# Row maxima of a sparse-attention block: the key products of the maximum pass on half the contraction rows

## The reference

```python
o_cmp, p_cmp = compressed_attention(q, kc, vc, scale)     # 63 compressed keys
sel_idx = select_blocks(p_cmp, s_len)                     # 16 of 16 blocks: all of them
o_slc = selected_attention(q, k_s, v_s, sel_idx, scale)   # causal over all keys
o_win = window_attention(q, k_w, v_w, scale)              # causal, last 512 keys
```

## Time and profile before

| | |
|---|---|
| median of 3 runs | 992.6 us (991.83 to 993.16) |
| the profiled execution | 991.09 us, its span 989.3 us |
| granted TensorE clock, mean | 0.987 |
| PE busy | 910.2 us (92%), 5573 products |
| DVE busy | 528.5 us (53%) |
| ACT busy | 394.5 us (40%) |
| chain that ended last, by engine | PE 71%, DVE 14%, ACT 6%, SP queue 3% |
| maximum pass | first product at 308.8 us, last at 594.0 us |

### The profile page before, as it was taken

One profiled execution on the slowest core, in us unless ns is written; L12 is line 12 of the kernel. 1 busy time (PEld: TensorE's weight loads), 2 busy tenths in 40 slices (PEclk: granted clock), 3 DMA queues, 4 the chain that ended last, 5 costly groups with the idle time before them and its releaser, 6 DMA issues.

```text
span 989.3 us, 14340 instructions
## 1 busy us (share of the span) xinstructions
PE 910.2 (92%) x5573; PEld 745.6 (75%) x5581; DVE 528.5 (53%) x1075; ACT 394.5 (40%) x786; POOL 215.7 (22%) x213
## 2 busy tenths in 40 slices
PE   0799999899999999999998998889999999999996
PEld 0488999689999766666676766678888888877885
DVE  1561279426765487797786876552231222217543
ACT  5533232422123466767657667641111111114121
POOL 6249512111100112212203212145551000000000
PEclk9999999899999999999999999989999999999998
DMA  9917041031010000000000001043322112033222
GB/s 314 356 44 128 4 111 65 1 88 45 1 44 1 2 1 1 1 1 1 2 1 1 1 2 32 7 123 96 100 71 70 53 33 59 16 154 127 87 85 85
DMA packets 53716, 59.67 MB, mean 60 GB/s; under 512 B 10097, under 2 KB 45489, under 8 KB 52609
## 3 DMA queue, kind: packets, MB, share of 16 engines
q1 hardware_dynamic: 51392, 54.13, 18.3%
q0 software_dynamic: 2000, 4.54, 1.6%
q10 hardware_dynamic: 256, 0.09, 0.0%
HBM read 52.92 MB, written 5.24 MB: 59 GB/s over the span
## 4 chain that ended last, share of the span: by engine, by line
PE 71%; DVE 14%; ACT 6%; SPq 3%; issue 3%; DMA 2%; POOL 0%; DVEq 0%; ACTq 0%; POOLq 0%
PE bank L1588 39%; PE slc_max L1588 15%; PE win_max L1588 13%; PE bank L1591 3%; DVE plo L1142 3%; SPq L488 2%; DVE rt L1142 2%; DVE mx L1410 2%; DMA ada<-in_w_ada 2%; ACT pt L815 1%; DVE mx L1417 1%; ACT phi L815 1%; ACT osb L815 1%; DVE qa L1142 1%; SPq L527 1%
## 5 line engine op out<-in xcount | busy, mean ns | idle before, releaser
L1142 DVE TENSOR_TENSOR plo<-pt,phi 128x512 fp32r<-128x512 f32 x192 | 116.2, 621 | 36.8 <-ACT phi L815 36.4
L815 ACT ACTIVATE pt<-bank 128x512 f32<-128x512 f32 (+1 forms) x208 | 98.7, 474 | 83.3 <-PE bank L1588 77.2
L1588 PE MATMUL bank<-q,k 128*128 128x512 f32 (+7 forms) x384 | 102.7, 349 | 0.9
L815 ACT ACTIVATE phi<-bank 128x512 fp32r<-128x512 f32 (+1 forms) x208 | 98.5, 474 | 0.0
L601 POOL TENSOR_TENSOR qa<-qa,otmp 128x256 f32<-128x256 f32 x32 | 27.5, 859 | 215.2 <-DVE otmp L1142 215.2
L1588 PEld LDWEIGHTS bank<-q,k 128*128 128x128 f32 (+1 forms) x384 | 63.4, 190 | 11.9 <-ACT phi L815 2.9
L1588 PE MATMUL bank<-phi,vhi 128*65 128x512 f32 x192 | 70.1, 365 | 2.4 <-ACT osb L815 1.9
L1588 PE MATMUL bank<-phi,vlo 128*64 128x512 f32 x192 | 62.0, 323 | 0.0
L1588 PE MATMUL bank<-plo,vhi 128*65 128x512 f32 x192 | 61.9, 323 | 0.0
L1588 PE MATMUL bank<-ht_hi,dhi 128*128 128x512 f32 x128 | 50.6, 396 | 2.8 <-DVE at_lo L1142 2.8
L1410 DVE TENSOR_REDUCE mx<-slc_max 128x1 f32<-128x128 f32 (+3 forms) x64 | 48.1, 752 | 8.7 <-PE slc_max L1588 8.7
(11 more groups left out here) (395 smaller groups left out, 2535.8 us busy)
## 6 DMA issues: line engine op xcount, KB each, us to landing
ada<-in_w_ada SPq DMA_DIRECT2D x8, 1024.0 KB, 17.0
draw<-in_w_in SPq DMA_DIRECT2D x16, 512.0 KB, 3.9
wraw<-in_w_in SPq DMA_DIRECT2D x7, 1024.0 KB, 5.4
xs<-in_x SPq DMA_DIRECT2D x8, 512.0 KB, 10.9
gstage<-in_w_ada POOLq DMA_DIRECT2D x16, 256.0 KB, 3.1
oraw<-in_w_out SPq DMA_DIRECT2D x8, 512.0 KB, 6.5
xr<-in_x SPq DMA_DIRECT2D x8, 512.0 KB, 4.3
out<-yr SPq DMA_DIRECT2D x8, 512.0 KB, 2.9
```

Of the source, the lines that this page charges most:

```text
L815: return nc.scalar.activation(o, i, fn, **kw)
L1142: return V.tensor_tensor(o, a, b, op)
L1588: return T.matmul(o, l, r, start=start, stop=stop, **kw)
```

## The change

The products of the maximum pass contract 64 rows instead of 128, that is query high part times key high part, without the key's low part. So that selected and window keys lie on different rows, the window keys' high part goes to slot 1 of `kcat` and their low part to slot 0: of the window's `k1`, rows 64 to 127 hold the high part. The copy into `k2` then reads rows 64 to 127 for the window. "MX" and "MW" become one step: both waits first, then in turn a selected product on rows 0 to 63 and a window product on rows 64 to 127, each in its own bank, then the masks of the selected keys (signal `ms`), the window's masks, the compressed mask, and the compressed product with all 128 rows last (signal `mw`). The "MW" entries stay in the plan; TensorE does nothing at them.

```diff
--- before.py
+++ after.py
@@ -1070,7 +1070,7 @@
                 act.wait_ge(once("krot"), m + 1)
                 if m >= 2:
                     act.wait_ge(s_tr, key_fill(m - 2) + 1)
-                a(kcat[m % 2][:, :, 0, :], rt1[:, 0:P].rearrange("p (g d) -> p g d", g=GROUPS))\
+                a(kcat[m % 2][:, :, m // ST, :], rt1[:, 0:P].rearrange("p (g d) -> p g d", g=GROUPS))\
                     .then_inc(once("khi"), 1)
                 if m >= 2:
                     key_high(m - 2)
@@ -1469,7 +1469,7 @@
                 dve.wait_ge(s_tr, fl + 1)
                 dve.wait_ge(once("k1"), m + 1)
                 V.tensor_copy(k2[b][0:HD, :, P * i:P * i + P],
-                              bank[fl % 2][0:HD, 0:2 * P].rearrange("p (g s) -> p g s", g=GROUPS))\
+                              bank[fl % 2][HD * b:HD * b + HD, 0:2 * P].rearrange("p (g s) -> p g s", g=GROUPS))\
                     .then_inc(s_trf, 1)
 
             for m in range(2 * ST):
@@ -1491,8 +1491,8 @@
                 dve.wait_ge(once("krot"), m + 1)
                 dve.wait_ge(once("khi"), m + 1)
                 kc_ = kcat[m % 2]
-                tt(kc_[:, :, 1, :], rt1[:, 0:P].rearrange("p (g d) -> p g d", g=GROUPS),
-                   f(kc_[:, :, 0, :]), ALU.subtract).then_inc(once("klo"), 1)
+                tt(kc_[:, :, 1 - b, :], rt1[:, 0:P].rearrange("p (g d) -> p g d", g=GROUPS),
+                   f(kc_[:, :, b, :]), ALU.subtract).then_inc(once("klo"), 1)
                 if m >= 2:
                     key_rows(m - 2)
                 if m == 2:
@@ -1888,27 +1888,21 @@
                     lhs = q1[h % 2][:, P * i:P * i + P]
                     if n >= 1:
                         pe.wait_ge(once("msr"), n)
-                    for s0 in range(0, i + 1, 4):
-                        s1 = min(s0 + 4, i + 1)
-                        mm(slc_max[:, P * s0:P * s1], lhs, k1[0][:, g, P * s0:P * s1], True, s1 != i + 1)
-                    mm(slc_max[:, P * i:P * i + P], identb[:, :], maskb[:, 0, :], False, True).then_inc(once("ms"), 1)
-                elif step[0] == "MW":
-                    _, h, i = step
-                    n, g = max_no(h, i), h // HPG
-                    lhs = q1[h % 2][:, P * i:P * i + P]
-                    buf = win_max
-                    if n >= 1:
                         pe.wait_ge(once("mwr"), n)
                     j0 = max(0, i - WIN_TILES)
                     cnt = i + 1 - j0
-                    for s0 in range(0, cnt, 4):
-                        s1 = min(s0 + 4, cnt)
-                        mm(buf[:, P * s0:P * s1], lhs, k1[1][:, g, P * (j0 + s0):P * (j0 + s1)], True, False)
+                    for s0 in range(0, i + 1, 4):
+                        s1, w1_ = min(s0 + 4, i + 1), min(s0 + 4, cnt)
+                        mm(slc_max[:, P * s0:P * s1], lhs[0:HD], k1[0][0:HD, g, P * s0:P * s1], True, s1 != i + 1)
+                        if s0 < cnt:
+                            mm(win_max[:, P * s0:P * w1_], lhs[HD:P], k1[1][HD:P, g, P * (j0 + s0):P * (j0 + w1_)],
+                               True, False)
+                    mm(slc_max[:, P * i:P * i + P], identb[:, :], maskb[:, 0, :], False, True).then_inc(once("ms"), 1)
                     if i >= WIN_TILES:
-                        mm(buf[:, 0:P], identb[:, :], maskb[:, 1, :], False, True)
-                    mm(buf[:, P * (cnt - 1):P * cnt], identb[:, :], maskb[:, 0, :], False, True)
-                    mm(buf[:, 640:704], lhs, k1c[:, g, 0, :], True, False)
-                    mm(buf[:, 640:704], identb[:, :], cmpq[:, i, :], False, True).then_inc(once("mw"), 1)
+                        mm(win_max[:, 0:P], identb[:, :], maskb[:, 1, :], False, True)
+                    mm(win_max[:, P * (cnt - 1):P * cnt], identb[:, :], maskb[:, 0, :], False, i < WIN_TILES)
+                    mm(win_max[:, 640:704], identb[:, :], cmpq[:, i, :], i < WIN_TILES, False)
+                    mm(win_max[:, 640:704], lhs, k1c[:, g, 0, :], False, True).then_inc(once("mw"), 1)
                 elif step[0] == "MM":
                     h, hf = step[1:]
                     pe.wait_ge(once("mcat"), 2 * (h + 1))
```

## The result

The median became 997.57 us (996.80 to 999.44) against 992.63 us for the kernel before, four runs each: ratio 1.0052, interval 1.0036 to 1.0068. The change costs 4.9 us, where 1.7 were forecast; the time lies inside the prediction's range (989.0 to 998.0) and outside the likeliest case's own (992.0 to 996.5). The profiled execution took 998.23 us, its span is 996.4, 7.1 us longer than before.

What follows compares the result with a forecast made beforehand. TensorE was taken as busy 35.96 of 38.65 us a head, alternating with VectorE on the chain. Heads +1.4 and opening +0.3 took 991.1 to 992.8 us; 1.5 more gave 994.3, range 989.0 to 998.0.

Steps and rivals of the forecast that it cites:

- likeliest case: The forecast of 994.3 us for the whole kernel, with its own range 992.0 to 996.5 and chance 0.60.
- The half form on TensorE: Maximum pass: two halves take the time of one, switches take 0.23 to 0.29 us back; tiles 4 to 7 -0.09 to -0.10.
- state-space rows: Trace rows of 64-row products in the state-space stage: two halves overlap fully, entering costs 0.19 us behind a plain product.
- Rival (a): Switches beside bf16 masks are cheaper: 986.6 us if they cost nothing, 990.5 half way; chance 0.17.
- The merged wait at tile 7: Tile 7's selected products also wait for tile 6's window maxima; TensorE's next columns come 0.34 us later a head.
- The slack on VectorE: VectorE's 0.54 us wait near 474.8 absorbs selected signals 0.2 us later, and output transposes find bank 7 free.
- Rival (b): VectorE's queue passes the later signal on: 0.22 us at tile 3, 0.23 at tile 4, 997.5 us; chance 0.18.
- Tile 2 was put under cover: Tile 2's +0.06 us on TensorE costs nothing, lying inside the VectorE stretch that ends at 463.93.
- The opening: Head 0's tiles, between projection blocks: plain entries on TensorE and later tiles waiting for maxima, together +0.3 us.
- The key preparation: Eight copies reading rows 64 to 127 and writing rows 0 to 63 cost 0; +3.3 us without VectorE's free time.
- The sum: Seven heads at +0.2 us give +1.4, with the opening's +0.3 making +1.7 us in all.
- that 1.5 us: The whole kernel's median before, 992.6 us, lay 1.5 above its profiled execution; the forecast added this to 992.8.

Runs made afterwards that it cites:

- e4_new45: The changed kernel with the half-height form at tiles 4 and 5 alone, all other tiles as before; 993.76 us against 991.99, ratio 1.0018.
- e1_waits: The kernel before with only the wait for the window maxima moved ahead of the first selected product; 997.91 us against 992.16, ratio 1.0073.
- e3_old67: The changed kernel with tiles 6 and 7 as before (128 rows, separate waits); 993.19 us against 992.16, ratio 1.0016.
- e2_signal: The kernel before; at tiles 0 to 5 the selected maxima's signal comes with the first window product; 997.04 us, ratio 1.0052; rerun 998.30 us, ratio 1.0056.
- e5_same_rows: The changed kernel with the key layout of before and all half-height products on rows 0 to 63; 1009.50 us, ratio 1.0176.
- e8_combo: The kernel before with the compressed product early at tiles 0 to 5, but half form at tiles 4 and 5 of heads 1 to 7; 991.35 us, ratio 0.9994.
- e7_comp_early: The kernel before with the compressed product between the selected products and their mask at tiles 0 to 5; 991.97 us against 991.99, ratio 1.0006.

## Why the prediction was 3.3 us too low, point by point

**The half form on TensorE: right.** Entering behind a mask (first half 0.16 us after it), the pair at once, leaving with 0.10 us, the tile 0.1 us shorter: all as forecast from the state-space rows. (Entering behind a plain product is 0.18 us by the prediction's own times, 160.58 to 160.76, not 0.19.) Tile 4→5 gave −0.10 in the changed kernel and −0.12 in e4_new45, forecast −0.09. Rival (a), free switches, is out.

**The merged wait at tile 7: right.** Forecast +0.34 a head, measured +0.37 (6→7 and 7→0); e1_waits and e3_old67 show it by itself.

**The slack on VectorE: the step that failed.** The prediction knew that each selected maximum would start about 0.2 us later, and took 0.54 us of idle time at 474.85 as the place where that is absorbed, and the transposes as free. They aren't. They wait for VectorE's product into `qa`, which stands in the same queue behind the maxima, ahead of that idle time and not behind it. Against the forecast distances the head has +0.14 at 2→3, +0.18 at 3→4 and +0.12 at 5→6, together 0.44 of the 0.45 us between its 38.85 and 39.30; the other distances cancel to 0.01. The three come about in different ways. At 3→4 it is the late signal of tile 3, straight through the queue to `qa` and the transposes. At 2→3 it is the late signal of tile 1, by the longer overlap with GpSimd, which no part of the prediction had. At 5→6 it is a term that the sum left out: the merged wait holds tile 6 too. Tile 5's window maxima end at 478.12 and tile 6 starts at 478.26, 0.31 us after the mask ahead of it instead of 0.16. That takes both parts of the change: e1_waits and e2_signal, each with one, have +0.01 there.

Rival (b) named the first of these, put +0.22 at tile 3 and +0.23 at tile 4, and gave 39.3 us a head and 997.5 us. Its 0.22 was about right (+0.18 at 3→4); its 0.23 did not come at tile 4, where 4→5 has the −0.10 of the forecast. That its head and its time are met to 0.1 us is in part luck: the overlap with GpSimd and the wait at tile 6 filled the gap in the head, and the opening made good what seven heads had less. The rows already spoke for its mechanism: the text wrote that `qa` "ends just ahead" of the transposes and that the case decides from a delay of 0.05 us there, had a delay of 0.2 us, and still gave it a chance of 0.18.

**Tile 2 was put under cover.** It was costed at nothing because VectorE's stretch, not TensorE, ends last there. For its own signal that was right, as shown above. But the stretch was taken as fixed, and it grew by 0.14 us: such a cover hides work of TensorE, and makes each lengthening on VectorE a delay of the head.

**The opening: +0.90 us measured, +0.3 forecast.** A third of the miss of 0.60 is arithmetic. The prediction's own terms are +0.08, +0.11, +0.06, 0, −0.03, and by the same steps +0.09 for tile 5 and +0.21 for tile 6: +0.52, not 0.3. (In one of them a slip of 0.03 is hidden: 0.75 and 1.96 make 2.71, not 2.68.) The rest has two parts. One is a step applied to too few tiles: the prediction let tile 7 wait for tile 6's maxima, and tile 6 for tile 5's, but not tile 5 for tile 4's. TensorE and VectorE there, in the changed kernel:

```profile
318.46 0.50 PE L1588 MATMUL slc_max<-k,q 64*128 64x512 f32 x1
...
320.65 0.28 PE L1588 MATMUL bank<-z1hi,ht_lo 128*128 128x256 f32 x1
321.05 0.47 PE L1588 MATMUL slc_max<-k,q 64*128 64x512 f32 x1
...
323.80 0.46 PE L1588 MATMUL slc_max<-k,q 64*128 64x512 f32 x1 [0.25 <-DVE mx L1417]
```

```profile
319.21 0.82 DVE L1410 TENSOR_REDUCE mx<-slc_max 128x1 f32<-128x640 f32 x1 [0.93 <-PE slc_max L1588]
...
320.09 0.81 DVE L1417 TENSOR_REDUCE mx<-win_max 128x1 f32<-128x640 f32 x1
```

Tile 4's maxima are out at 320.90, and tile 5 starts at 321.05, after the last projection product at 320.65 had left TensorE free at 320.77. A half product starts 0.15 us after the signal that it waited for, here and at tile 7 (481.05 to 481.20), where a full one started 0.05 after it (477.41 to 477.46). That is the other part: the forecast had kept the 0.05. The three waiting tiles give 2.59, 2.75 and 2.93 us where it had 2.43, 2.62 and 2.81: +0.41, and the tiles ahead of them 0.03 less than forecast.

**The key preparation: nothing seen, 0 was right.** The part of the span ahead of the pass is 0.82 us longer in the changed kernel's execution, but its two stretches at the lower clock level are 6.8 us each where the kernel before has 3.4 and 6.8. e1_waits, with the key preparation of before, has 6.8 and 6.8 too and reaches the pass at 309.72 us, the changed kernel at 309.64. e5_same_rows (as before) and e8_combo (turned) have 6.8 and 3.4 and reach it at 309.53 and 309.56. The 1.28 us behind the pass is such a difference as well: with one stretch of 10.2 instead of 6.8 us there the changed kernel takes 386.62 us and e1_waits 386.60; before it is 385.34.

**The sum.** 7 heads at 0.59 on average (4.14 over the stretch behind the opening) and 0.90 of opening are the pass's 5.04 us, and the median moved by 4.9. The forecast had 1.4 and 0.3. So the heads make 2.7 us of the miss and the opening 0.6, and these two alone give the 3.3. Two more terms cancel by luck: the changed kernel's profiled execution has 2.1 us more outside the pass, where 0 was forecast, and its time is 0.7 us above the median, where the forecast put the median 1.5 us above it, as before. Adding that 1.5 us took a chance of one execution's clock for a constant.

## What to carry to other kernels

When two waits are merged, or a signal comes later, don't look for the receiving engine's next idle time, but for the next signal that this engine sends: what stands between the late work and that signal passes the delay on. Look also at what runs beside it: a moved instruction can meet another engine's, as the split met GpSimd's product here. A wait moved ahead of a queue is best tried alone first; here one added wait cost as much as the whole change, and leaving it out at the two tiles that stand closest together (e3_old67) gave back 0.53 of 0.65 us a head. Half-height products pay where a tile is wide enough for two at once to outweigh 0.23 us of switching (tiles 4 and 5: 0.12 us each in the pass, which the kernel's median did not show).

## What was not expected of the hardware

**A lower clock outside the changed code.** TensorE's granted clock is 1.00 all through the heads, but the engine falls to its lower level, 1.2 GHz, for single stretches of 3.4 to 10.2 us before and behind the pass, and their number and length change from one execution to the next. Busy times and clock of 640 to 660 us in the kernel before and after:

```profile
640.00:660.00 20.00, 15.17 (x62) 12.22 (x63) 11.86 (x15) 10.32 (x14) 8.48 (x7) 0.83 0.52 146
```

```profile
640.00:660.00 20.00, 14.76 (x74) 12.00 (x74) 14.09 (x22) 10.94 (x17) 7.51 (x6) 0.74 0.36 100
```

Before, one stretch of 6.8 us at the lower level, after, one of 10.2 us; in both TensorE was busy about 15 of the 20 us. Runs of one kernel line up with their mean clock: the kernel of e2_signal took 993.2 us at 0.987, 996.5 at 0.982 and 998.3 to 999.1 at 0.979. This is worth 5 to 6 us, as much as the whole change. How many runs have a mean clock of 0.983 or below differs by kernel: none of 51 of before, nine of eleven of e2_signal's, seven of ten of e4_new45's, and fewer of the others (none of four of e5_same_rows', one of four of the changed kernel's and of e1_waits', one of ten of e3_old67's, three of twelve of e7_comp_early's, two of eleven of e8_combo's). Why is open. A gain of 1 to 2 us in the pass (e4_new45, e7_comp_early, e8_combo) therefore can't be read from a median; it was read from the pass's length in the trace. Runs at the same mean clock point the same way: at 0.984 e8_combo took 990.8 to 991.8 us (seven runs) and before beside it 992.5 to 994.4 (three).

**GpSimd slows a two-operand VectorE instruction** from 0.68 to 0.94, 1.06 or 1.09 us, by how far they overlap (0.40, 0.51 and 0.54 us), so a shift in time of VectorE's queue changes the length of its instructions too.
